# Two transformer blocks in fp32: the feed-forward up product as one 512-column product over both parts of the tokens, in four banks, with the gate product on GpSimd

## The chip, the core and the metric

One NeuronCore of a Trainium2 chip runs the whole program in one launch. The time is device microseconds from start to end of an execution; the profile gives a span, from the first instruction to the last. TensorE (PE) multiplies, VectorE (DVE), ScalarE (ACT) and GpSimd (POOL) do the elementwise work, SyncE (SP) issues all loads. PEld is TensorE's loading of the stationary operand, which overlaps its products.

## What is computed

256 tokens of width 1024 pass through a first block (an RWKV-7 and a dilated-attention mixer, then a gated feed-forward) and two layers of a second block, each with a feed-forward, a sparse-attention mixer and another feed-forward. That makes five feed-forwards. Cut to what matters here:

```python
D_FF = -(-8 * D_MODEL // (3 * 256)) * 256          # 2816

# first block
h = modulate(rms_norm(x, g_pre_ffn[i]), shift_f, scale_f)
u, gt = jnp.split(h @ w_ffn_in[i], 2, axis=-1)
f = (jax.nn.silu(u) * gt) @ w_ffn_out[i]
x = x + gate_f[:, None, :] * rms_norm(f, g_post_ffn[i])

# second block, twice in each of two layers
def swiglu(h, w13, w2):
    a, b = jnp.split(h @ w13, 2, axis=-1)
    return (jax.nn.silu(a) * b) @ w2
```

All of it is in float32.

## The kernel before

**Split products.** The feed-forward's products take operands of type fp32r. Each operand is split into a high part (ACT's copy into fp32r) and a low part (what that copy leaves of the fp32 value), and three products are added: high times high, high times low, low times high. For a feed-forward, the normed tokens `hT` are split once into `h_hi` and `h_lo`, and every weight is split as it arrives: ACT copies it into the high part (`high_up`, L1546; `high_down`, L1554), DVE subtracts to get the low part (`low_up`, L1984; L2006).

**Chunks.** The 2816 hidden channels are worked in FC = 11 chunks of 256. A chunk's up weights (2 MB, in one of two `ring` slots) hold 256 channels of u and 256 of the gate: four output tiles j of 128 channels (0 and 1 are u, 2 and 3 the gate). Each tile needs eight k-steps over the width of 1024, so a chunk has 32 of them. They come in two halves h of four k-steps, since `up_hi` and `up_lo` hold the weights of one half each: the second half is split while the first is multiplied. A k-step is three products of 256 columns (the tokens), L881, L882 and L883, each with a weight load of its own. The `down` products of a chunk (24 of 512 columns, L897 to L899) add onto banks 0 to 3 through all chunks.

**PSUM.** A chunk's up results take two banks, u in one and the gate in the other; even chunks use banks 4 and 5, odd ones 6 and 7. Chunk 0 is done unsplit (L854).

**Order.** Each engine runs its instructions in the order in which they are written, and waits on semaphores. PE's is up(0), up(1), down(0), up(2), down(1), up(3), ..., up(10), `down_end`. Before up(c) it waits for the gate product of the chunk that used the same banks (`act_ready`). For chunk c, in its loop:
- ACT: high part of the next chunk's first half (after the first half of up(c)); silu of u from PSUM (L1565); high part of the next chunk's second half; high part of the down weights (after down(c-1)).
- DVE: low part of the next chunk's first half; gate product from PSUM (L1995); high and low part of it (`act_hi` L1999, `act_lo` L2001); low part of the next chunk's second half; low part of the down weights (L2006); and, in the first four feed-forwards, four dot products for the conditioning vector of a later layer (`ada_layers`, L1953).

In `down_end`, PE multiplies half of chunk 9's down product, waits for `act_low` of chunk 10, runs eight products (L907, L908), waits for `dn_low`, and goes on (L910); then come norm, residual and the next stage, all of which wait for these sums. POOL has nothing to do in a feed-forward but the residual's add at its end (L2621). SP loads the up weights, the down weights and the dot products' weights in turn, each when its buffer is free.

Of the kernel before, what the change touches and what calls it, by code (L numbers as in the profile page):

```python
# [28 lines left out]
ACT = mybir.ActivationFunctionType  # L29
ALU = mybir.AluOpType  # L30
# [4 lines left out]
S = 256  # L35
NT = S // P
KD = D // P
FF = 2816
FC = FF // 256
# [239 lines left out]
def build(nc, T, out):  # L279
    with ExitStack() as ctx:  # L280
# [3 lines left out]
        def sem(name):  # L284
            return ctx.enter_context(nc.semaphore(name))
# [17 lines left out]
        silu = scratch[:, 1024:2048].rearrange("p (b n) -> p b n", b=2)  # L303
        fin = scratch[:, 2048:3072].rearrange("p (t n) -> p t n", t=2)
        with nc.sbuf_tensor("row_split", [P, D], F32R) as row_split:
            pass
# [22 lines left out]
        arena = sb("arena", [P, ARENA])  # L329
        h_hi, h_lo = (split[:, a:a + 2048].rearrange("p (k n) -> p k n", k=KD) for a in (0, 2048))  # L330
        up_hi, up_lo = (split[:, a:a + 4096].rearrange("p (h n) -> p h n", h=2) for a in (4096, 8192))
# [117 lines left out]
        up_high = sem("up_high")  # L449
        up_low = sem("up_low")  # L450
        dn_high = sem("dn_high")
        dn_low = sem("dn_low")
# [371 lines left out]
        def _(pe):  # L824
# [19 lines left out]
            def ffn_split(f, n, g):  # L844
# [21 lines left out]
                def up(c, i=0):  # L866
                    if c >= 2:
                        pe.wait_ge(act_ready, FC * f + c + i - 1)
                    if c == 0:
                        up_first()  # L870
                        return
                    if c == 1:
                        pe.wait_ge(h_low, 2 * (f + 1))
                    for h in range(2):
                        pe.wait_ge(up_low, up_count(f, c, h) + 2 * i)
                        for j in range(4):

                            dst = bank[4 + 2 * (c % 2) + j // 2][:, (j % 2) * S:(j % 2 + 1) * S]
                            for k in range(4):
                                a, kt_ = slice(k * 512 + j * P, k * 512 + j * P + P), 4 * h + k  # L880
                                mm(dst, up_hi[:, h, a], h_hi[:, kt_], start=(kt_ == 0 and j % 2 == 0), stop=False, skip_group_check=True)  # L881
                                mm(dst, up_hi[:, h, a], h_lo[:, kt_], start=False, stop=False, skip_group_check=True)  # L882
                                last = mm(dst, up_lo[:, h, a], h_hi[:, kt_], start=False, stop=(kt_ == KD - 1), skip_group_check=True)  # L883
                        last.then_inc(half_done, 1)
# [653 lines left out]
        def _(act):  # L1538
# [17 lines left out]
            def ffn_split(f, g):  # L1556

                def one(c, i=0):
                    if c < FC - 1:
                        high_up(f, g, c + 1, 0, i)  # L1560
                    if c == 0:
                        high_up(f, g, 1, 1)
                    act.wait_ge(half_done, 2 * FC * f + 2 * (c + 1) + 2 * i)
                    wait(act, act_ready, FC * f + c + i - 1 if c >= 2 else FC * f)
                    F(silu[:, c % 2], bank[4 + 2 * (c % 2)], ACT.Silu).then_inc(silu_ready, 1)  # L1565
                    if 0 < c < FC - 1:
                        high_up(f, g, c + 1, 1, i)
                    high_down(f, c, i)

                one(0)  # L1570
                one(1)
                if f == 0:
                    act.wait_ge(ang_ready, 1)
                    F(sin2[:], sin2[:], ACT.Sin)
                    F(cos2[:], cos2[:], ACT.Sin).then_inc(trig_ready, 1)
                with act.Fori(0, FC - 3, 2) as i:
                    one(2, i)
                    one(3, i)
                one(FC - 1)
# [366 lines left out]
        def _(dve):  # L1946
# [39 lines left out]
            def ffn_split(f, g, n, mods):  # L1986

                def one(c, i=0):
                    if c < FC - 1:
                        low_up(f, g, c + 1, 0, i)  # L1990
                    if c == 0:
                        low_up(f, g, 1, 1)
                    dve.wait_ge(silu_ready, FC * f + c + i + 1)
                    whole = act_t[:, c % 2].rearrange("p k n -> p (k n)")
                    tt(whole, silu[:, c % 2], bank[5 + 2 * (c % 2)], ALU.mult).then_inc(act_ready, 1)  # L1995
                    dve.wait_ge(act_ready, FC * f + c + i + 1)
# [4 lines left out]
                    tt(act_lo[:, c % 2], whole, act_hi[:, c % 2].bitcast(F32), ALU.subtract).then_inc(act_low, 1)  # L2001
                    if 0 < c < FC - 1:
                        low_up(f, g, c + 1, 1, i)
                    d_hi, d_lo = (up_hi[:, 1], up_lo[:, 1]) if c == FC - 1 else (dn_hi, dn_lo)
# [591 lines left out]
        def _(pool):  # L2596
# [20 lines left out]
            def add(n):  # L2617

                for t in range(NT):
                    pool.wait_ge(fin_read, 4 * n + 2 * t + 1)  # L2620
                    tt(x[:, t, 0:512], x[:, t, 0:512], fin[:, 0], ALU.add).then_inc(x_ready, 1)  # L2621

            def angles():

# [134 lines left out]
            add(0)  # L2759
            angles()  # L2760
            add(1)

            g(pool.memset(zb, 0.0))
            pool.memset(lf8, 0.0).then_inc(pool_zero, 1)

            for l in range(LAYERS):
                add(2 + 3 * l)
                channel_major(T2, CM_2 + 16 * l, Q1 + Q2 * l, range(14))
                for p in range(NP):
# [4 lines left out]
                    for e in range(2):  # L2774
# [3 lines left out]
                        last.then_inc(p_ready, 1)  # L2778
                add(3 + 3 * l)
                add(4 + 3 * l)  # L2780

# [17 lines left out]
```

## Time and profile before

| | |
|---|---|
| time, median of 3 runs | 1678.69 us (1675.34 to 1680.26) |
| span of the profiled execution | 1675.9 us |
| PE busy, mean granted clock over the span | 96%, 0.993 |
| the five feed-forwards from chunk 1 to the end of up(10) | 426 to 592, 622 to 788, 961 to 1126, 1154 to 1319, 1492 to 1658 us |

No time of its own is given for the profiled execution beside its span; the median lies 2.8 us above the span, and a difference worked out on the trace is applied to the median. A matmul's row shows a start and a modelled end, and products overlap: what one costs in a stream is the distance from its start to the next one's. "Busy" of PE thus says that it had work, not how fast it went. A row's "idle before" names what ended the wait.

### The profile page before, as it was taken

The numbers are of one execution on the slowest core, as the hardware profiler recorded it, in microseconds if no ns is written. First come the engines' busy times: TensorE is split into PE (matmuls) and PEld (weight loads), VectorE is DVE, ScalarE is ACT, GpSimd is POOL, SyncE is SP. The second block draws the span as 40 slices with busy tenths as digits, with TensorE's granted clock in tenths as the row PEclk, the third lists the DMA queues.
The fourth block names the chain that finished last, engine by engine and source line by source line (L and its number), as shares of the span: only waits on it lengthen the run. The fifth ranks groups of instructions, "written<-read, shape, count | busy, mean of one in ns | idle before, by whom it ended". The sixth has DMA issues, their size and how long they took to land.

```text
span 1675.9 us, 31948 instructions
## 1 busy us (share of the span) xinstructions
PE 1604.4 (96%) x13122; PEld 1447.5 (86%) x13122; DVE 1112.0 (66%) x1812; ACT 681.3 (41%) x1026; POOL 234.3 (14%) x291
## 2 busy tenths in 40 slices
PE   3999988999999999999999999999999999999998
PEld 3998778785999989999896899999999888699997
DVE  5986445474777767787657577876877666755554
ACT  3443423302433353333457433335333354743333
POOL 0531345032300000000016000000000002500000
PEclk9999979999999999999999999999999999999999
DMA  9963110276778829786640488765887563164531
GB/s 393 347 231 126 51 53 4 70 278 240 298 290 324 329 86 347 307 309 242 220 173 2 166 342 330 289 269 212 315 328 289 222 201 118 56 236 162 218 152 61
DMA packets 59544, 363.90 MB, mean 217 GB/s; under 512 B 14000, under 2 KB 14768, under 8 KB 39472
## 3 DMA queue, kind: packets, MB, share of 16 engines
q1 hardware_dynamic: 59440, 362.42, 56.9%
q8 instruction: 76, 1.25, 0.3%
q14 instruction: 28, 0.23, 0.1%
HBM read 361.32 MB, written 1.08 MB: 216 GB/s over the span
## 4 chain that ended last, share of the span: by engine, by line
PE 84%; DVE 7%; issue 3%; DMA 2%; ACT 2%; POOL 2%; SPq 0%; POOLq 0%; DVEq 0%; ACTq 0%
PE psum L883 11%; PE psum L882 11%; PE psum L881 11%; PE psum L897 5%; PE psum L898 5%; PE psum L899 5%; PE psum L854 4%; PE psum L950 2%; PE psum L1051 2%; PE psum L987 2%; PE psum L988 2%; PE psum L989 2%; DMA arena<-in_ada_head 2%; PE psum L1339 1%; PE psum L1340 1%
## 5 line engine op out<-in xcount | busy, mean ns | idle before, releaser
L881 PE MATMUL psum<-split 128*128 128x256 f32 x1600 | 453.0, 283 | 0.0
L883 PE MATMUL psum<-split 128*128 128x256 f32 x1600 | 452.8, 283 | 0.0
L882 PE MATMUL psum<-split 128*128 128x256 f32 x1600 | 452.8, 283 | 0.0
L882 PEld LDWEIGHTS psum<-split 128*128 128x128 f32 x1600 | 307.0, 192 | 1.8
L881 PEld LDWEIGHTS psum<-split 128*128 128x128 f32 x1600 | 307.0, 192 | 1.7
L883 PEld LDWEIGHTS psum<-split 128*128 128x128 f32 x1600 | 307.0, 192 | 0.0
L1984 DVE TENSOR_TENSOR split<-ring,split 128x2048 fp32r<-128x2048 f32 x100 | 228.6, 2290 | 70.9 <-ACT split L1546 67.4
L1546 ACT ACTIVATE split<-ring 128x2048 fp32r<-128x2048 f32 x100 | 190.8, 1912 | 192.9 <-PE psum L883 141.8
L2006 DVE TENSOR_TENSOR split<-ring_down,split 128x2048 fp32r<-128x2048 f32 x55 | 126.2, 2294 | 106.2 <-ACT split L1554 106.2
L1953 DVE CUSTOM_DVE_ANT_0 arena<-arena,c_row 128x1024 f32<-128x1024 f32 x144 | 167.6, 1220 | 0.0
L2621 POOL TENSOR_TENSOR x_res<-x_res,scratch 128x512 f32<-128x512 f32 x16 | 20.6, 1286 | 999.6 <-DVE scratch L2044 798.3
L1554 ACT ACTIVATE split<-ring_down 128x2048 fp32r<-128x2048 f32 x55 | 105.4, 1916 | 133.4 <-PE psum L899 133.4
L897 PE MATMUL psum<-split 128*128 128x512 f32 x400 | 156.3, 391 | 0.0
L898 PE MATMUL psum<-split 128*128 128x512 f32 x400 | 156.2, 391 | 0.0
L899 PE MATMUL psum<-split 128*128 128x512 f32 x400 | 155.6, 389 | 0.0
L1565 ACT ACTIVATE scratch<-psum 128x512 f32<-128x512 f32 x55 | 32.9, 598 | 209.9 <-PE psum L883 202.4
L899 PEld LDWEIGHTS psum<-split 128*128 128x128 f32 x400 | 75.1, 188 | 16.0
L897 PEld LDWEIGHTS psum<-split 128*128 128x128 f32 x400 | 75.3, 188 | 14.3
L898 PEld LDWEIGHTS psum<-split 128*128 128x128 f32 x400 | 75.3, 188 | 13.8
L854 PE MATMUL psum<-hT,ring 128*128 128x128 f32 x640 | 73.4, 275 | 4.8 <-DVE hT L2065 4.8
L1995 DVE TENSOR_TENSOR scratch<-scratch,psum 128x512 f32<-128x512 f32 x55 | 37.8, 687 | 60.3 <-ACT scratch L1565 60.3
L854 PEld LDWEIGHTS psum<-hT,ring 128*128 128x128 f32 x640 | 72.4, 192 | 6.0 <-issue 4.1
(446 smaller groups left out, 3020.6 us busy)
## 6 DMA issues: line engine op xcount, KB each, us to landing
ring<-in_up SPq DMA_DIRECT2D x55, 2048.0 KB, 10.2
arena<-in_ada SPq DMA_DIRECT2D x168, 512.0 KB, 6.4
ring_down<-in_down SPq DMA_DIRECT2D x55, 1024.0 KB, 4.9
ring<-in_in SPq DMA_DIRECT2D x19, 2048.0 KB, 8.9
ring<-in_gates SPq DMA_DIRECT2D x4, 2048.0 KB, 8.5
arena<-in_ada_head SPq DMA_DIRECT2D x4, 1536.0 KB, 18.7
ring_down<-in_w_out SPq DMA_DIRECT2D x3, 2048.0 KB, 12.4
ring<-in_w_out SPq DMA_DIRECT2D x3, 2048.0 KB, 11.0
```

The source lines that it names most:

```text
L854: last = mm(dst, w[:, k * 512 + j * P:k * 512 + j * P + P], hT[:, k, t * P:(t + 1) * P], start=(t == 0 and k == 0 and j % 2 == 0), stop=(k ...
L881: mm(dst, up_hi[:, h, a], h_hi[:, kt_], start=(kt_ == 0 and j % 2 == 0), stop=False, skip_group_check=True)
L882: mm(dst, up_hi[:, h, a], h_lo[:, kt_], start=False, stop=False, skip_group_check=True)
L883: last = mm(dst, up_lo[:, h, a], h_hi[:, kt_], start=False, stop=(kt_ == KD - 1), skip_group_check=True)
L897: mm(bank[2 * t + h], act_hi[:, c % 2, a], dn_hi[:, w], start=(c == 0 and k == 0), stop=False, skip_group_check=True)
L898: mm(bank[2 * t + h], act_hi[:, c % 2, a], dn_lo[:, w], start=False, stop=False, skip_group_check=True)
L899: last = mm(bank[2 * t + h], act_lo[:, c % 2, a], dn_hi[:, w], start=False, stop=False, skip_group_check=True)
L1546: F(up_hi[:, h], ring[:, (g + c) % 2, h * 2048:(h + 1) * 2048], ACT.Copy).then_inc(up_high, 1)
L1554: F(up_hi[:, 1] if c == FC - 1 else dn_hi, ring_down[:, c % 2], ACT.Copy).then_inc(dn_high, 1)
L1953: return dve.tensor_tensor_reduce(out=weights, in0=weights, in1=c_of, scale=1.0, scalar=0.0, op0=ALU.mult, op1=ALU.add, accum_out=out)
L1984: tt(up_lo[:, h], ring[:, (g + c) % 2, h * 2048:(h + 1) * 2048], up_hi[:, h].bitcast(F32), ALU.subtract).then_inc(up_low, 1)
L2006: tt(d_lo, ring_down[:, c % 2], d_hi.bitcast(F32), ALU.subtract).then_inc(dn_low, 1)
```

## The change

- PE: `h_hi` and `h_lo` now lie side by side for each k (`h_both`). A k-step is one product of the high weights with both parts (512 columns, a whole bank) and one of the low weights with the high part (256 columns, onto the first half of the same bank). The four tiles j of a chunk take banks 4 to 7, one each, so all chunks use the same four; the first half of each bank holds two of the three products, the second half the third (high weights times low tokens).
- ACT copies the second halves of the four banks to SBUF (`up_whole`, 1024 columns), waits for DVE, and takes silu from SBUF.
- DVE adds the four first halves onto that copy (`up_sum`), and moves the low part of the next weights (`low_up`) ahead of `act_hi`. It no longer does the gate product.
- POOL does the gate product from SBUF (`ffn_gated`).
- PE waits for `up_sum` of the chunk before, where it waited for the gate product of the one before that. Chunk 0 keeps its old path; in up(1) the tiles go 2, 3, 0, 1, with a wait for chunk 0's gate product ahead of tile 0.

```diff
@@ buffers
+        up_whole = scratch[:, 2048:3072]
...
-        h_hi, h_lo = (split[:, a:a + 2048].rearrange("p (k n) -> p k n", k=KD) for a in (0, 2048))
+        h_both = split[:, 0:4096].rearrange("p (k s n) -> p k s n", k=KD, s=2)
+        h_hi, h_lo = h_both[:, :, 0], h_both[:, :, 1]
@@ PE, up(c)
                     if c >= 2:
-                        pe.wait_ge(act_ready, FC * f + c + i - 1)
+                        pe.wait_ge(up_sum, (FC - 1) * f + c + i - 1)
...
-                        for j in range(4):
-
-                            dst = bank[4 + 2 * (c % 2) + j // 2][:, (j % 2) * S:(j % 2 + 1) * S]
+                        for j in ((2, 3, 0, 1) if c == 1 and h == 0 else range(4)):
+                            if c == 1 and h == 0 and j == 0:
+                                pe.wait_ge(act_ready, FC * f + 1)
                             for k in range(4):
                                 a, kt_ = slice(k * 512 + j * P, k * 512 + j * P + P), 4 * h + k
-                                mm(dst, up_hi[:, h, a], h_hi[:, kt_], start=(kt_ == 0 and j % 2 == 0), stop=False, skip_group_check=True)
-                                mm(dst, up_hi[:, h, a], h_lo[:, kt_], start=False, stop=False, skip_group_check=True)
-                                last = mm(dst, up_lo[:, h, a], h_hi[:, kt_], start=False, stop=(kt_ == KD - 1), skip_group_check=True)
+                                mm(bank[4 + j], up_hi[:, h, a], h_both[:, kt_].rearrange("p s n -> p (s n)"),
+                                   start=(kt_ == 0), stop=(kt_ == KD - 1), skip_group_check=True)
+                                last = mm(bank[4 + j][:, 0:S], up_lo[:, h, a], h_hi[:, kt_], start=False, stop=(kt_ == KD - 1), skip_group_check=True)
@@ ACT, one(c)
-                    wait(act, act_ready, FC * f + c + i - 1 if c >= 2 else FC * f)
-                    F(silu[:, c % 2], bank[4 + 2 * (c % 2)], ACT.Silu).then_inc(silu_ready, 1)
+                    if c == 0:
+                        wait(act, act_ready, FC * f)
+                        F(silu[:, 0], bank[4], ACT.Silu).then_inc(silu_ready, 1)
+                    else:
+                        act.wait_ge(act_ready, FC * f + c + i)
+                        F(up_whole.rearrange("p (j n) -> p j n", j=4), psum[:, 4:8, S:2 * S], ACT.Copy).then_inc(low_out, 1)
+                        act.wait_ge(up_sum, (FC - 1) * f + c + i)
+                        F(silu[:, c % 2], up_whole[:, 0:512], ACT.Silu).then_inc(silu_ready, 1)
@@ DVE, one(c)
-                    dve.wait_ge(silu_ready, FC * f + c + i + 1)
                     whole = act_t[:, c % 2].rearrange("p k n -> p (k n)")
-                    tt(whole, silu[:, c % 2], bank[5 + 2 * (c % 2)], ALU.mult).then_inc(act_ready, 1)
+                    if c == 0:
+                        dve.wait_ge(silu_ready, FC * f + 1)
+                        tt(whole, silu[:, 0], bank[5], ALU.mult).then_inc(act_ready, 1)
+                    else:
+                        dve.wait_ge(low_out, (FC - 1) * f + c + i)
+                        four = up_whole.rearrange("p (j n) -> p j n", j=4)
+                        tt(four, four, psum[:, 4:8, 0:S], ALU.add).then_inc(up_sum, 1)
+                        if c < FC - 1:
+                            low_up(f, g, c + 1, 1, i)
                     dve.wait_ge(act_ready, FC * f + c + i + 1)
...
-                    if 0 < c < FC - 1:
-                        low_up(f, g, c + 1, 1, i)
@@ POOL, new, called for each feed-forward
+            def ffn_gated(f):
+
+                def one(c, i=0):
+                    pool.wait_ge(silu_ready, FC * f + c + i + 1)
+                    if c >= 2:
+                        pool.wait_ge(act_low, FC * f + c + i - 1)
+                    else:
+                        wait(pool, act_low, FC * f)
+                    tt(act_t[:, c % 2].rearrange("p k n -> p (k n)"), silu[:, c % 2], up_whole[:, 512:1024], ALU.mult).then_inc(act_ready, 1)
+
+                one(1)
+                with pool.Fori(0, FC - 3, 2) as i:
+                    one(2, i)
+                    one(3, i)
+                one(FC - 1)
```

The start of up(1) in PE's own order, behind the unsplit products of up(0), before:

```order
L854 MATMUL psum<-hT,ring 128x128 x31
L881 MATMUL psum<-split 128x256 [waits up_low,h_low]
L882 MATMUL psum<-split 128x256
L883 MATMUL psum<-split 128x256
L881 MATMUL psum<-split 128x256
L882 MATMUL psum<-split 128x256
L883 MATMUL psum<-split 128x256
```

and after:

```order
L858 MATMUL psum<-hT,ring 128x128 x31
L885 MATMUL psum<-split 128x512 [waits up_low,h_low]
L887 MATMUL psum<-split 128x256
L885 MATMUL psum<-split 128x512
L887 MATMUL psum<-split 128x256
```

Six products of 256 columns for two k-steps became two of 512 and two of 256.

DVE's order over one chunk of the loop (`split<-ring` is `low_up`, `scratch<-scratch,psum` reads the up result, `split<-scratch` are `act_hi` and `act_lo`, `split<-ring_down` is the down weights' low part), before:

```order
L1984 TENSOR_TENSOR split<-ring,split 128x2048 [waits up_high]
L1993 REGISTER_ALU
L1995 TENSOR_TENSOR scratch<-scratch,psum 128x512 [waits silu_ready]
L1998 REGISTER_ALU [waits act_ready]
L1999 CAST split<-scratch 128x512 [waits down_done]
L2001 TENSOR_TENSOR split<-scratch,split 128x512 [waits act_high]
L1983 REGISTER_ALU
L1984 TENSOR_TENSOR split<-ring,split 128x2048 [waits up_high]
L2006 TENSOR_TENSOR split<-ring_down,split 128x2048 [waits dn_high]
```

and after:

```order
L1994 TENSOR_TENSOR split<-ring,split 128x2048 [waits up_high]
L2010 TENSOR_TENSOR scratch<-scratch,psum 128x1024 [waits low_out]
L1993 REGISTER_ALU
L1994 TENSOR_TENSOR split<-ring,split 128x2048 [waits up_high]
L2013 REGISTER_ALU
L2016 CAST split<-scratch 128x512 [waits down_done,act_ready]
L2018 TENSOR_TENSOR split<-scratch,split 128x512 [waits act_high]
L2021 TENSOR_TENSOR split<-ring_down,split 128x2048 [waits dn_high]
```

The 512-column product became a 1024-column sum that waits for ACT's copy, and the second `low_up` now stands right behind it.

ACT's order over the last chunk of the loop and the end of a feed-forward (`split<-ring` is `high_up`, `split<-ring_down` is `high_down`), before:

```order
L1546 ACTIVATE split<-ring 128x2048 [waits half_done]
L1563 REGISTER_ALU
L1565 ACTIVATE scratch<-psum 128x512 [waits act_ready,half_done]
L1546 ACTIVATE split<-ring 128x2048 [waits half_done]
L1553 REGISTER_ALU [waits down1_full]
L1554 ACTIVATE split<-ring_down 128x2048 [waits down_done]
L1576 REGISTER_ALU
L1576 COMPARE_AND_BRANCH
L1565 ACTIVATE scratch<-psum 128x512 [waits act_ready,half_done]
L1554 ACTIVATE split<-ring_down 128x2048 [waits half_done,down0_full]
```

and after:

```order
L1550 ACTIVATE split<-ring 128x2048 [waits half_done]
L1567 REGISTER_ALU
L1572 REGISTER_ALU [waits half_done]
L1573 ACTIVATE scratch<-psum 128x1024 [waits act_ready]
L1575 ACTIVATE scratch<-scratch 128x512 [waits up_sum]
L1550 ACTIVATE split<-ring 128x2048 [waits half_done]
...
L1586 REGISTER_ALU
L1586 COMPARE_AND_BRANCH
L1573 ACTIVATE scratch<-psum 128x1024 [waits act_ready,half_done]
L1575 ACTIVATE scratch<-scratch 128x512 [waits up_sum]
L1558 ACTIVATE split<-ring_down 128x2048 [waits half_done,down0_full]
```

Where one silu stood between the two `high_up`, there are now a copy, a wait for DVE's sum and a silu; the same at the end, ahead of `high_down`.

## Rows read from the trace of the kernel before

**Rows 1.** The page, part 1: busy time by engine.

```profile
PE 1604.4 (96%) x13122; PEld 1447.5 (86%) x13122; DVE 1112.0 (66%) x1812; ACT 681.3 (41%) x1026; POOL 234.3 (14%) x291
```

**Rows 2.** The page, part 4: the chain that ended last, by engine.

```profile
PE 84%; DVE 7%; issue 3%; DMA 2%; ACT 2%; POOL 2%; SPq 0%; POOLq 0%; DVEq 0%; ACTq 0%
```

**Rows 3.** Busy time in the five feed-forward blocks: the line that sums the stretches.

```profile
sum 828.00, PE 828.00 PEld 783.95 DVE 581.59 ACT 297.19 POOL 9.44; mean PE 165.60 PEld 156.79 DVE 116.32 ACT 59.44 POOL 1.89
```

**Rows 4.** Timeline of PE, first block: start us, us, then the instruction.

```profile
488.81 0.40 PE L897 MATMUL psum<-split 128*128 128x512 f32 x1
...
494.28 0.28 PE L881 MATMUL psum<-split 128*128 128x256 f32 x1
...
505.79 0.40 PE L897 MATMUL psum<-split 128*128 128x512 f32 x1
...
507.18 0.39 PE L897 MATMUL psum<-split 128*128 128x512 f32 x1
```

**Rows 5.** Timeline of PE in the second block's mixer: products of 284 columns.

```profile
830.72 0.29 PE L1353 MATMUL psum<-split 128*128 128x284 f32 x1
...
836.72 0.29 PE L1354 MATMUL psum<-split 128*128 128x284 f32 x1
```

**Rows 6.** Timeline of DVE, one chunk of the second feed-forward.

```profile
652.67 0.43 DVE L1999 CAST split<-scratch 128x512 fp32r<-128x512 f32 x1
...
653.74 2.28 DVE L1984 TENSOR_TENSOR split<-ring,split 128x2048 fp32r<-128x2048 f32 x1
658.57 2.29 DVE L2006 TENSOR_TENSOR split<-ring_down,split 128x2048 fp32r<-128x2048 f32 x1 [2.54 <-ACT split L1554]
660.77 1.22 DVE L1953 CUSTOM_DVE_ANT_0 arena<-arena,c_row 128x1024 f32<-128x1024 f32 x1
...
665.70 2.29 DVE L1984 TENSOR_TENSOR split<-ring,split 128x2048 fp32r<-128x2048 f32 x1
```

**Rows 7.** Timeline of ACT, the same chunk.

```profile
651.23 0.60 ACT L1565 ACTIVATE scratch<-psum 128x512 f32<-128x512 f32 x1 [3.19 <-PE psum L883]
651.72 1.91 ACT L1546 ACTIVATE split<-ring 128x2048 fp32r<-128x2048 f32 x1
```

**Rows 8.** Single lines: count, then duration ns min/median/max, first and last start.

```profile
L1670 ACT ACTIVATE raw<-psum x54: 362/386/388, 41.7 to 1416.0; 128x256 f32<-128x256 f32 x54
L1995 DVE TENSOR_TENSOR scratch<-scratch,psum x55: 679/687/690, 427.2 to 1657.6; 128x512 f32<-128x512 f32 x55
L2301 DVE TENSOR_SCALAR arena<-psum x1: 1757/1757/1757, 324.7 to 324.7; 128x1536 f32<-128x1536 f32 x1
L2621 POOL TENSOR_TENSOR x_res<-x_res,scratch x16: 1267/1288/1299, 395.3 to 1667.9; 128x512 f32<-128x512 f32 x16
L2607 POOL TENSOR_TENSOR pre<-raw x20: 616/1193/1720, 42.2 to 93.9; 128x256 f32<-128x256 f32 x20
```

**Rows 9.** Timeline of ACT, DVE and PE at the first block's end.

```profile
590.89 0.60 ACT L1565 ACTIVATE scratch<-psum 128x512 f32<-128x512 f32 x1 [9.60 <-PE psum L883]
591.59 0.69 DVE L1995 TENSOR_TENSOR scratch<-scratch,psum 128x512 f32<-128x512 f32 x1 [2.52 <-ACT scratch L1565]
592.31 0.43 DVE L1999 CAST split<-scratch 128x512 fp32r<-128x512 f32 x1
593.38 2.28 DVE L2006 TENSOR_TENSOR split<-ring_down,split 128x2048 fp32r<-128x2048 f32 x1
595.72 0.50 PE L910 MATMUL psum<-split 128*128 128x512 f32 x1
```

**Rows 10.** Timeline of PE and DVE, start of the fourth block's loop.

```profile
1165.49 0.40 PE L897 MATMUL psum<-split 128*128 128x512 f32 x1
1169.28 0.68 DVE L1995 TENSOR_TENSOR scratch<-scratch,psum 128x512 f32<-128x512 f32 x1
```

**Rows 11.** Timeline of PE in the first mixer, then windows with granted clock (PEclk).

```profile
221.53 0.68 PE L1189 MATMUL psum<-arena 64*64 64x64 f32 x16 [2.55 <-POOL arena L2708]
...
226.00:242.00 16.00, 15.98 (x259) 14.92 (x260) 7.71 (x21) 5.35 (x13) 7.83 (x11) 0.50 0.02 3
```

More of the change, by code:

```diff
@@ L450, in build @@
         up_low = sem("up_low")
+        low_out = sem("low_out")
+        up_sum = sem("up_sum")
         dn_high = sem("dn_high")
@@ L2760, in _ @@
             angles()
+            ffn_gated(0)
             add(1)
@@ L2766, in _ @@
             for l in range(LAYERS):
+                ffn_gated(1 + 2 * l)
                 add(2 + 3 * l)
@@ L2779, in _ @@
                 add(3 + 3 * l)
+                ffn_gated(2 + 2 * l)
                 add(4 + 3 * l)
```

## Prediction

> **What bounds the kernel now.** I read the busy times first: PE has work for 1604.4 of 1675.9 us [rows 1], and the chain that ended last is 84% PE [rows 2]. In the five feed-forward blocks PE is never without work, 828.00 of 828.00 us, while DVE has 581.59 and ACT 297.19 [rows 3]. So in the loop the time is the number of products times their distance, and an engine beside PE counts only if it makes PE wait. What one costs I take from starts in a stream [rows 4]. From L897 at 488.81 to L881 at 494.28 lie 24 down products, 5.47 us, 227.9 ns each; from there to L897 at 505.79 lie the 96 up products of 256 columns, 11.51 us, 119.9 ns each. A chunk takes 16.98 us. Twice the columns cost 108.0 ns more and not 119.9: some 12 ns come with each product, whatever its width. The 284-column products agree: 46 distances in 6.00 us, 130.4 ns, which is 10.5 ns more for 28 more columns (columns alone, at 108.0 ns for 256, would make 11.8) [rows 5]. The weight load isn't that charge, since a 512-column product has twice the time to hide it and pays it too.
>
> The exception is a block's end. There PE has only 12 products to do while silu, gate product, both parts of it and the low down weights are made one after another: silu at 590.89, gate product 591.59, `act_hi` 592.31, low down weights 593.38, and L910 starts at 595.72 when they are done [rows 9]. All that follows hangs on this chain, five times.
>
> **The change part by part.**
>
> *Products.* A k-step was 3 x 119.9 = 359.7 ns and becomes 227.9 + 119.9 = 347.8, or 11.9 less. There are 32 k-steps in a chunk, 10 split chunks, 5 feed-forwards: 1600, so -19.0 us, and a chunk takes 16.60 us. The mixed stream isn't in the trace. Its bounds: the first six down products behind up products stand 1.39/6 = 231.7 ns apart, and the later ones less, (494.28 - 488.81 - 1.39)/18 = 226.7 [rows 4]. If every 512 pays the first, a k-step is 351.6 and the saving 13.0 us; at the second, 346.6 and 21.0. I take the mean of a whole down block, between them.
>
> *The way from up(c) to up(c+1) in the loop.* Before, up(c+1) used other banks. Now it waits for the sum over the same ones, behind down(c-1), which gives 5.47 us of cover. What must fit: ACT's copy of 1024 columns, DVE's sum of 1024. ACT reads 256 from PSUM in 386 ns [rows 8] and 512 in 0.60 us [rows 7], 214 ns per 256, so 1.03 for 1024; above, two separate 512s make 1.20. DVE takes 0.687 for 512 and 1.757 for 1536 [rows 8], so 1.22 for 1024; above, 2 x 0.687 = 1.37. With an allowance of 0.35 for three hand-overs it is done 2.6 us after up(c), 2.9 before PE needs it. Cost nothing, while DVE is free at that moment.
>
> *Is it?* DVE now goes round in a closed loop: sum 1.27 with its hand-over; silu to `high_up` on ACT 0.49 and `high_up` 1.94 with hand-over [rows 7], in which DVE waits; `low_up` 2.20 (distance 658.57 to 660.77 of the same size); `act_hi` and `act_lo` 1.07 (652.67 to 653.74); low down weights 2.20; dot products 4.93 (660.77 to 665.70); `low_up` 2.20 [rows 6]. Sum 16.30 against PE's 16.60: 0.3 us per chunk to spare, 0.15 with the sum at its upper bound. The fifth block has no dot products. It also starts late in a block, when chunk 2's weights are still landing: in the worst, the fourth, DVE gets to its PSUM work at 1169.28, where down starts at 1165.49 [rows 10]. After: sum done 1170.55, PE there at 1165.49 - 0.38 + 5.47 = 1170.58. Just covered; price 0, at most 0.2. If the cover goes, each 0.1 us of DVE loop over 16.60 costs up to 36 x 0.1 us.
>
> POOL's product falls into DVE's wait for `high_up` and takes 1.29 alone [rows 8]; with chunks to spare before down(c) it costs nothing in the loop. The moved `low_up` ends 7.3 us behind up(c), needed at 5.47 + 5.56. SP issues the loads behind the same DVE steps, some 0.8 us later in each chunk; DMA is 2% of the chain [rows 2], and the buffers are two deep, so I count nothing for it.
>
> *Block end.* Here each added step is on the path [rows 9]. Out go silu to gate product 0.70 and gate product to `act_hi` 0.72: 1.42. In come copy 1.03, sum 1.22, silu 0.60, POOL's product 1.29 (L2621's, the same size [rows 8]) and four hand-overs, 0.30: 4.44. The rest is unchanged, and so L910 starts 3.02 us later in relation to up(10)'s end. Five times: +15.1 us. Bounds: 1.20 and 1.37 for the reads give +16.7; without hand-overs +13.6. Nothing starts earlier for it: DVE and ACT are both idle there before.
>
> *Chunk 0 and up(1):* tile 0 waits for chunk 0's gate product, done about 1.6 us after up(0), behind 8 k-steps (2.8 us). Nothing.
>
> **Sum:** -19.0 + 15.1 = -3.9 us. On the span 1675.9 that is 1672.0; on the median 1678.69 it is 1674.8, say 1675. With all bounds, -21.0 + 13.6 = -7.4 to -13.0 + 16.7 + 0.2 = +3.9. A measurement here tells about 0.3% or 5.0 us from no change, so the likeliest case lies within it, and reaches beyond on the faster side only.
>
> **Rivals.**
>
> *The charge isn't saved (slower).* The 12 ns may go with the work and not with the product: a mixed stream then costs 359.7 ns per k-step as before, and only the end's +15.1 is left: 1694. For it: no row has 512 and 256 in turn. Against: three widths fit one charge per product [rows 4, 5]. The Trainium skill (TensorE: Matmul & The Clock Gate, Back-to-back issue gap) gives columns over 2.4 GHz plus 2.5 ns, by which a merged product saves 2.5 ns; an estimate by it is -4.0 + 15.1 = +11.1 us, 1690. The trace disagrees on the charge, with 12.
>
> *PE's clock falls at the block ends (slower).* PE's 12 products (2.7 us) begin with the silu at 590.9 at the latest and are over by 593.6, about when `act_low` is made before (L2006 follows it at 593.38 [rows 9]); now it comes 3.02 later, and PE stands for about 3 us. In the first mixer it waited 2.55 us before 221.53, with little work ahead of that, and ran at half clock (0.50) through 226 to 242 [rows 11]. Behind the wait stand 36 products of 227.9 ns, 8.2 us; if half of them run at 1.2 GHz instead of 2.4 it is +4.1 us a block. One such fall cancels the gain; from three on the kernel is slower by over 0.3%; all five give +16.6, 1695. Against: here PE was full before and is full right after. By the same page (Part 1) an idle array is clocked down and a busy one gets its clock back; the trace shows both, at 222 and 244 us.
>
> *DVE's loop or POOL is slower than reckoned.* A loop of 16.9 instead of 16.30 makes PE wait 0.3 in most of 36 chunks, +8 after what slack there is: +4.1, 1683. Or POOL's product takes twice its time at the ends, +6.5: +2.6, 1681. POOL rows do range from 616 to 1720 ns for one size [rows 8]. Either stays within 0.3% of before; both together, or a loop over 16.95, are slower.
>
> *More is saved.* If in the mixed stream the short product's charge is hidden too (107.9 for 119.9), a further 19 us go: -23, 1656. PE would then need 16.2 us a chunk, DVE's loop of 16.30 takes over in four blocks (36 x 0.1 us back), and about -20 remains: 1659. For it I see only that the distance changes by 5 ns within a down block [rows 4].
>
> **Chances.** The forecast 0.64, charge not saved 0.06, clock 0.09, DVE or POOL 0.13, more saved 0.08. Of the forecast's range, -7.4 to +3.9 around -3.9, three eighths lie beyond -5.0. Faster by over 0.3%: 0.24 + 0.08 = 0.32. Slower: 0.06 + 0.06 + 0.05, and 0.02 for the forecast's tail: 0.19. Within: 0.49. The likeliest case's own range is 1671 to 1683. The range that should hold 8 in 10 takes in most of the rivals in the middle and leaves out "more saved" and the clock falling at four ends or more: 1668 to 1687.
>
> **What the profile would show.** Right: starts of L885 to L887 about 228 ns apart and of L887 to the next L885 about 120; a chunk of 16.6 us; PE busy through the loop with no wait on `up_sum`; copy 1.03, sum 1.22, POOL's product 1.29; L910 7.85 us after ACT's copy starts at a block's end, where it is 4.83 after the silu's start now. Wrong: PE waiting on DVE's sum L2010 in the loop, PEclk under 1 behind the ends, or other distances in the mixed stream. That last one is the largest unknown: each 5 ns per k-step are 8 us.

## The result: 0.6% slower, and the profile after

The changed kernel takes 1689.53 us in the median of 4 runs (1684.74 to 1692.5), the kernel before 1679.16 beside it; the ratio is 1.0058, with a 95% interval of 1.0042 to 1.0073, or 9.7 us more. The forecast was 1675.0 in a range of 1668 to 1687. The profiled execution is the fastest of the four (span 1683.0, mean granted clock 0.991; the others 0.987 to 0.989). Three single executions further down, far longer than all others (two of the kernel before, one of e6), count in no ratio, but the one of e6 is in its median of 1683.65.

Busy times of the page, after, which answer to [rows 1]:

```profile
PE 1597.1 (95%) x11522; PEld 1363.2 (81%) x11522; DVE 1134.1 (67%) x1812; ACT 733.5 (44%) x1076; POOL 299.1 (18%) x341
```

There are 1600 products fewer, but PE is busy only 7.3 us less, in a longer span. The first place to look is the loop. The timeline of ACT after, in the second feed-forward, gives the length of a chunk by the starts of its PSUM copy:

```profile
666.41 1.03 ACT L1573 ACTIVATE scratch<-psum 128x1024 f32<-128x1024 f32 x1 [3.80 <-PE psum L887]
683.20 1.03 ACT L1573 ACTIVATE scratch<-psum 128x1024 f32<-128x1024 f32 x1 [3.80 <-PE psum L887]
699.99 1.03 ACT L1573 ACTIVATE scratch<-psum 128x1024 f32<-128x1024 f32 x1 [3.80 <-PE psum L887]
```

A chunk takes 16.79 us: 0.19 less than the 16.98 of [rows 4], where 0.38 less was forecast. PE is never without work in it; this is the sum over five stretches inside the five blocks, to set beside [rows 3]:

```profile
sum 807.00, PE 807.00 PEld 688.34 DVE 595.92 ACT 336.80 POOL 67.50; mean PE 161.40 PEld 137.67 DVE 119.18 ACT 67.36 POOL 13.50
```

So the products themselves stand further apart than forecast. PE's timeline in the mixed stream:

```profile
655.18 0.40 PE L885 MATMUL psum<-split 128*128 128x512 f32 x1
655.41 0.28 PE L887 MATMUL psum<-split 128*128 128x256 f32 x1
655.53 0.40 PE L885 MATMUL psum<-split 128*128 128x512 f32 x1
...
656.59 0.40 PE L885 MATMUL psum<-split 128*128 128x512 f32 x1
```

From 655.18 to 656.59 lie four k-steps, 353 ns each; over a chunk's 32 it is 352.8 (11.29 us). In the mean of the whole trace 117 ns of it go to the product of 256 columns and 236 to that of 512. Forecast were 347.8, and at most 351.6. The down products behind the mixed stream are a little dearer too, 5.50 us for 24 where they took 5.47.

One place in the five blocks does wait, though a busy PE hides it (timeline of DVE and PE, first chunk of the fourth block's loop):

```profile
1173.02 1.21 DVE L2010 TENSOR_TENSOR scratch<-scratch,psum 128x1024 f32<-128x1024 f32 x1
1173.98 0.39 PE L903 MATMUL psum<-split 128*128 128x512 f32 x1
1174.37 0.49 PE L885 MATMUL psum<-split 128*128 128x512 f32 x1
```

DVE's sum ends at 1174.23, and L885 starts 0.39 us behind L903 instead of 0.23; that chunk takes 17.07 us, 0.28 more than the others. It is the tight spot that the prediction named, and it costs this once.

The end of the first block, which answers to [rows 9] (timeline after; starts and durations in us, then the instruction):

```profile
586.71 1.03 ACT L1573 ACTIVATE scratch<-psum 128x1024 f32<-128x1024 f32 x1 [9.31 <-PE psum L887]
587.84 1.22 DVE L2010 TENSOR_TENSOR scratch<-scratch,psum 128x1024 f32<-128x1024 f32 x1 [2.04 <-ACT scratch L1573]
589.09 0.63 ACT L1575 ACTIVATE scratch<-scratch 128x512 f32<-128x512 f32 x1 [1.36 <-DVE scratch L2010]
589.80 1.27 POOL L2646 TENSOR_TENSOR scratch<-scratch 128x512 f32<-128x512 f32 x1 [15.41 <-ACT scratch L1575]
591.11 0.43 DVE L2016 CAST split<-scratch 128x512 fp32r<-128x512 f32 x1 [2.04 <-POOL scratch L2646]
592.17 2.28 DVE L2021 TENSOR_TENSOR split<-ring_down,split 128x2048 fp32r<-128x2048 f32 x1
592.31 0.50 PE L911 MATMUL psum<-split 128*128 128x512 f32 x1 [2.86 <-DVE split L2018]
594.51 0.50 PE L914 MATMUL psum<-split 128*128 128x512 f32 x1
```

L914 (L910 before) starts 7.80 us behind the copy; 7.85 was forecast, and it was 4.83 behind the silu before. PE now stands idle for 2.86 us, and does so in all five blocks (waits of PE: line, releaser, total us, times, longest):

```profile
PE psum L911 <- DVE split L2018: 14.2, 5, 2.9
```

Behind that idle the granted clock falls in three of the five blocks. The second block's end, PE's timeline and two windows (the value before the DMA share is the clock):

```profile
789.49 0.80 PE L911 MATMUL psum<-split 128*128 128x512 f32 x1 [2.86 <-DVE split L2018]
790.08 0.63 PE L912 MATMUL psum<-split 128*128 128x512 f32 x1
...
791.36 0.63 PE L911 MATMUL psum<-split 128*128 128x512 f32 x1
```

```profile
788.00:792.00 4.00, 2.52 (x6) 2.03 (x7) 3.32 (x3) 2.18 (x3) 0.24 (x1) 0.59 0.02 4
792.00:796.00 4.00, 4.00 (x11) 3.11 (x11) 1.38 (x2) 0.00 (x0) 1.00 (x1) 0.55 0.00 0
```

The products stand 427 ns apart (790.08 to 791.36, three distances) where they stood 227: about half speed, the lower level of 1.2 GHz. From the copy at 783.88 to L914 at 793.07 it takes 9.19 us, 1.39 more than in the first block, and the four L914 products are slow as well (+0.8).

Block by block, the time from the first product behind up(10) to the 48th (all but the last few at the block's end) has grown by 2.98, 4.67, 3.97, 2.98 and 4.15 us against the trace before. So the longer chain costs 2.98 each time, and the lower clock 1.7, 1.0 and 1.2 us in the second, third and fifth block: 3.9 in this execution. A further fall, at 604 to 608 us (clock 0.57), lies behind a later wait, the one for the next stage's transposes; the kernel before has none there.

### The profile page after: what moved, and what is told of

Same layout as the page of the kernel before. It is cut to its first block, busy times and chain, and to the rows that moved or that the text cites. A ratio compares the mean times of both kernels' runs of the same rounds, so it can differ in the third digit from the quotient of the medians.

```text
span 1683.0 us, 29059 instructions
## 1 busy us (share of the span) xinstructions
PE 1597.1 (95%) x11522; PEld 1363.2 (81%) x11522; DVE 1134.1 (67%) x1812; ACT 733.5 (44%) x1076; POOL 299.1 (18%) x341
## 4 chain that ended last, share of the span: by engine, by line
PE 83%; DVE 7%; issue 3%; DMA 3%; ACT 2%; POOL 2%; SPq 0%; POOLq 0%; DVEq 0%; ACTq 0%
PE psum L885 22%; PE psum L887 11%; PE psum L901 5%; PE psum L903 5%; PE psum L902 5%; PE psum L858 4%; PE psum L954 2%; PE psum L1055 2%; DMA arena<-in_ada_head 2%; PE psum L1343 1%; PE psum L1344 1%; PE psum L1345 1%; PE psum L991 1%; PE psum L992 1%; PE psum L993 1%
## 5 line engine op out<-in xcount | busy, mean ns | idle before, releaser
L885 PE MATMUL psum<-split 128*128 128x512 f32 x1600 | 566.9, 398 | 0.0
L887 PE MATMUL psum<-split 128*128 128x256 f32 x1600 | 449.1, 281 | 0.0
L885 PEld LDWEIGHTS psum<-split 128*128 128x128 f32 x1600 | 300.6, 188 | 74.2 <-issue 0.4
L887 PEld LDWEIGHTS psum<-split 128*128 128x128 f32 x1600 | 302.1, 189 | 1.7
L2646 POOL TENSOR_TENSOR scratch<-scratch 128x512 f32<-128x512 f32 x50 | 64.7, 1294 | 826.7 <-ACT scratch L1575 826.7
L901 PE MATMUL psum<-split 128*128 128x512 f32 x400 | 157.5, 394 | 0.0
L903 PE MATMUL psum<-split 128*128 128x512 f32 x400 | 156.5, 391 | 0.0
L902 PE MATMUL psum<-split 128*128 128x512 f32 x400 | 156.1, 390 | 0.0
L1573 ACT ACTIVATE scratch<-psum 128x1024 f32<-128x1024 f32 x50 | 51.4, 1028 | 193.0 <-PE psum L887 192.9
L903 PEld LDWEIGHTS psum<-split 128*128 128x128 f32 x400 | 75.2, 188 | 17.3
L901 PEld LDWEIGHTS psum<-split 128*128 128x128 f32 x400 | 75.2, 188 | 16.5
L902 PEld LDWEIGHTS psum<-split 128*128 128x128 f32 x400 | 75.3, 188 | 14.5
L2010 DVE TENSOR_TENSOR scratch<-scratch,psum 128x1024 f32<-128x1024 f32 x50 | 60.9, 1218 | 37.8 <-ACT scratch L1573 37.7
L1575 ACT ACTIVATE scratch<-scratch 128x512 f32<-128x512 f32 x50 | 31.6, 632 | 87.6 <-DVE scratch L2010 87.6
L1963 DVE CUSTOM_DVE_ANT_0 arena<-arena 128x1024 f32<-128x1024 f32 x40 | 52.0, 1318 | 15.7 <-DMA arena<-in_ada_head 15.5
```

What stands on the lines that cost most here:

```text
L885: mm(bank[4 + j], up_hi[:, h, a], h_both[:, kt_].rearrange("p s n -> p (s n)"), start=(kt_ == 0), stop=(kt_ == KD - 1), skip_group_check=True)
L887: last = mm(bank[4 + j][:, 0:S], up_lo[:, h, a], h_hi[:, kt_], start=False, stop=(kt_ == KD - 1), skip_group_check=True)
L901: mm(bank[2 * t + h], act_hi[:, c % 2, a], dn_hi[:, w], start=(c == 0 and k == 0), stop=False, skip_group_check=True)
L902: mm(bank[2 * t + h], act_hi[:, c % 2, a], dn_lo[:, w], start=False, stop=False, skip_group_check=True)
L903: last = mm(bank[2 * t + h], act_lo[:, c % 2, a], dn_hi[:, w], start=False, stop=False, skip_group_check=True)
L1963: return dve.tensor_tensor_reduce(out=weights, in0=weights, in1=c_of, scale=1.0, scalar=0.0, op0=ALU.mult, op1=ALU.add, accum_out=out)
```

## The experiments

All ratios are against the kernel before, run on the same chip; 0.1% is 1.7 us.

| kernel | us, median | ratio, 95% interval | chunk in the loop, us |
|---|---|---|---|
| changed kernel | 1689.53 | 1.0058 (1.0042 to 1.0073) | 16.79 |
| e1, last chunk the old way | 1669.92 | 0.9943 (0.9931 to 0.9956) | 16.79 |
| e2, only last chunk new | 1697.14 | 1.0109 (1.0092 to 1.0126) | 16.98 |
| e3, grouped by width | 1678.31 | 0.9997 (0.9988 to 1.0007) | 16.57 |
| e4, filler at the ends | 1683.5 | 1.0029 (1.0018 to 1.0039) | 16.79 |
| e5, e1 and e3 together | 1660.14 | 0.9879 (0.9863 to 0.9896) | 16.57 |
| e6, grouped by four | 1683.65 | 1.0021 (1.0011 to 1.0031) | 16.69 |
| e7, staggered | 1684.32 | 1.0027 (1.0017 to 1.0038) | 16.72 |
| e8, e5 with gate product on DVE | 1685.27 | 1.0030 (1.0019 to 1.0040) | 16.57 to 17.55 |
| e9, e5 with fewer passages | 1660.61 | 0.9887 (0.9871 to 0.9903) | 16.55 |
| e10, real work in the idle | 1690.49 | 1.0064 (1.0042 to 1.0086) | 16.79 |

**e1 and e2: the middle against the end.** In e1, chunk 10 keeps the form of before; its silu and gate product read PSUM directly:

```diff
+ if c == FC - 1:
+     dst = bank[4 + j // 2][:, (j % 2) * S:(j % 2 + 1) * S]
+     mm(dst, up_hi[:, h, a], h_hi[:, kt_], ...)
+     mm(dst, up_hi[:, h, a], h_lo[:, kt_], ...)
+     last = mm(dst, up_lo[:, h, a], h_hi[:, kt_], ...)
+     continue
```

> Chunks 1 to 9 of each block in the new form, chunk 10 as in the kernel before. Theory A (the mixed stream saves only 6.4 ns a k-step, 359.7 to 353.3; the 3.0 us at each block's end come from the longer chain behind the last chunk; the clock falls come from the idle that this chain leaves): 1440 k-steps x 6.4 ns = 9.2 us saved, no added chain, no falls: 9 us less than before, about 1670, ratio 0.9945, chunk period 16.79 us, PE waiting under 0.1 us ahead of the last down block, granted clock 1.00 at all five ends. Rival B (the added work on ScalarE, VectorE and GpSimd holds the loop up, so that the chunks of the middle carry part of the loss): 1675 or more and a period over 16.8 us. Rival C (the charge is not saved at all): 1679, as before.

Measured: 9.6 us less than before, with a chunk of 16.79 us (45 x 0.19 would be 8.6; the interval reaches from 7.4 to 11.6). Of L911's wait nothing is left, and no window behind a wait at a block's end has a clock under 1.00.

e2 is the reverse: only chunk 10 takes the new form.

> Chunks 1 to 9 as before, only chunk 10 of each block in the new form. Theory A: five chains of +3.0 us = +15.1, less 160 k-steps x 6.4 ns = 1.0, plus what the clock falls cost (0 to 6 us): 1693 to 1699, ratio 1.0085 to 1.012; L914 again 7.8 us behind the copy's start and PE idle 2.9 us ahead of it. If the loss came from the loop of the middle chunks instead (rival B), it would be near before: 1679 to 1684.

Measured: 18.3 us more than before, 4.2 beyond the 15.1 - 1.0 expected without falls of the clock. PE waits at the ends as after (waits of PE in e2, then windows behind the second, third, fourth and fifth block):

```profile
PE psum L917 <- DVE split L2025: 14.2, 5, 2.9
```

```profile
796.00:800.00 4.00, 3.11 (x9) 2.46 (x10) 3.00 (x3) 1.59 (x3) 0.00 (x0) 0.74 0.00 0
1140.00:1144.00 4.00, 4.00 (x13) 3.14 (x12) 1.89 (x3) 0.00 (x0) 0.06 (x1) 0.66 0.00 0
1336.00:1340.00 4.00, 4.00 (x12) 3.14 (x13) 2.46 (x2) 0.67 (x2) 0.00 (x0) 0.66 0.00 0
1680.00:1684.00 4.00, 4.00 (x15) 3.17 (x14) 1.29 (x3) 0.07 (x1) 1.29 (x1) 0.75 0.00 0
```

The clock falls here with 45 of 50 chunks in the old stream: the falls come with the idle, not with the mixed products. Middle and end are two separate effects, and the end is the loss.

**e4 and e10: the clock.** e4 adds twelve products ahead of the wait; their values are dropped:

```diff
  down_half(FC - 2, 0)
+ pe.wait_ge(up_sum, (FC - 1) * (f + 1))
+ for _ in range(12):
+     mm(bank[5], act_hi[:, 1, 0:P], dn_hi[:, 0:512], start=True, stop=True, ...)
  pe.wait_ge(act_low, FC * f + FC)
```

> The changed kernel with 12 products of 512 columns into bank 5 (free by then, their values are dropped) in the stretch in which TensorE waits at each block's end, behind the sum of chunk 10. Theory A (the idle of 2.86 us makes the granted clock fall): TensorE idles 0.2 us instead of 2.86 ahead of L911 of after, the clock stays 1.00 at all five ends, every run is near 1684 and their spread is below 2 us; the chain's 3.0 us stay. Rival (the falls have another cause, such as the load of the mixed stream): falls stay at the ends and the median is 1689 to 1691 as after.

Measured: 1683.5. Timeline of PE at the first block's end (L923 are the filling products), and windows there:

```profile
591.85 2.90 PE L923 MATMUL psum<-split 128*128 128x512 f32 x12
594.89 0.50 PE L911 MATMUL psum<-split 128*128 128x512 f32 x1
```

```profile
588.00:592.00 4.00, 4.00 (x21) 3.32 (x20) 1.54 (x4) 1.38 (x2) 0.00 (x0) 1.00 0.00 0
592.00:596.00 4.00, 3.86 (x18) 2.84 (x17) 2.28 (x3) 3.67 (x5) 1.30 (x1) 1.00 0.02 4
596.00:600.00 4.00, 3.92 (x18) 2.90 (x17) 1.67 (x4) 1.56 (x5) 0.00 (x0) 1.00 0.00 0
```

PE does useless work instead of standing, on the same chain, and the kernel is 0.29% (4.9 us, by the two ratios) faster than the changed one. The clock stays at 1.00 behind all five ends. One fall is left, later, at 604 to 612 us, where PE waits for the next stage's transposes, as after. The spread was not below 2 us as expected but 5 (1682.29 to 1687.4; eight of nine runs within 2.5). That 2.86 us of idle costs more than 2.86 us is what the Trainium skill (TensorE: Matmul & The Clock Gate, Part 1) leads one to look for, since by it an idle array is clocked down; this case's rows agree, though not in every block.

e10 puts real work in that place, chunk 9's products for the second 128 tokens:

```diff
  down_half(FC - 2, 0)
+ down_half(FC - 2, 1).then_inc(down_done, 1)
  pe.wait_ge(act_low, FC * f + FC)
...
- down_half(FC - 2, 1).then_inc(down_done, 1)
```

> The changed kernel with real work in place of the fillers of e4: the 12 products of chunk 9 for the second 128 tokens stand ahead of the wait for chunk 10's low part instead of behind its products for the first 128. TensorE no longer idles ahead of L911 of after, but what follows hangs on the first 128 tokens' chain, which starts as late as before the edit, so the 2.8 us come back as idle ahead of the transposes (L841, idle 1.0 to 3.8 us). Expected: as e4, 1683.5, if the clock stays up, 1686 to 1690 if it now falls behind the later idle; the gain of the full 2.7 us a block, 1671 to 1676, only if the second tokens' chain is what the next stage waits for.

Measured: 1690.49. The idle and the fall have only moved, ahead of and behind the next stage's transposes (timeline, then windows of e10; the clock is under 1 there in all five blocks):

```profile
608.01 1.97 PE L841 MATMUL psum<-const,xn 128*128 128x128 f32 x8 [3.67 <-DVE xn L2045]
```

```profile
608.00:612.00 4.00, 2.44 (x10) 2.06 (x11) 1.48 (x5) 2.74 (x9) 0.00 (x0) 0.50 0.92 327
612.00:616.00 4.00, 4.00 (x21) 4.00 (x21) 2.92 (x5) 2.50 (x6) 2.41 (x3) 0.50 0.00 0
```

The work to bring forward would have to be that of the first 128 tokens, on which all that follows hangs; it is the work that waits.

**e3, e6, e7, e9: where the other half of the saving went.** e3 gives the same products in another order (in outline):

```diff
- for j in ...: for k in range(4): 512 columns, 256 columns
+ for j in ...: for k in range(4): 512 columns
+ for j in ...: for k in range(4): 256 columns
```

> The changed kernel with the products of each half chunk regrouped: 16 of 512 columns, then 16 of 256 (2 changes of width instead of 32); the block ends are as after. Theory D (the dear product is a charge of about 6.5 ns per change back to 512 columns): 346.6 + 0.4 ns per k-step, 6.3 ns x 1600 = 10 us less than after, about 1679. Theory E (a run-in: the first six or so 512-column products of a group cost 233 ns, the rest 226.7, as in the down blocks): 4 ns x 1600 = 6.5 us less than after, about 1683. Theory F (512-column products with these weights cost 233.6 ns whatever stands between them): as after, 1689.5.

Measured: 1678.31, 0.6% under the changed kernel. PE's timeline of e3, a chunk's four groups (the third in the row that begins it: 16 products of each width per half):

```profile
655.05 3.79 PE L886 MATMUL psum<-split 128*128 128x512 f32 x16
658.68 2.08 PE L891 MATMUL psum<-split 128*128 128x256 f32 x16
660.59 3.82 PE L886 MATMUL psum<-split 128*128 128x512 f32 x16
664.25 2.08 PE L891 MATMUL psum<-split 128*128 128x256 f32 x16
666.16 0.40 PE L905 MATMUL psum<-split 128*128 128x512 f32 x1
```

A product of 512 columns takes 3.63/16 = 226.9 ns, one of 256 takes 1.91/16 = 119.4, and a k-step (666.16 - 655.05)/32 = 347.2. These are close to the forecast's numbers (347.8; 16.60 us a chunk, here 16.57). So the 12 ns do go with each product, and the merger saves them; the alternation of widths gives about half back.

e6 groups by four (one tile: 4 of 512, 4 of 256), e7 lets each 256-column product lag its partner by four, so that it adds to another bank:

> The changed kernel with the products of one tile regrouped by four: 4 of 512 columns, then 4 of 256, into the same bank. Mixed stream: 353.3 ns a k-step with 16 changes of width and back in a half chunk; grouped: 347.2 with one. A charge of 6.5 ns per change gives 346.8 + 6.5/4 = 348.4 ns, a period near 16.63 us and 1681. A run-in of several products behind each change leaves all four at the dear price: 353 ns, 16.79 us, 1689.

> The changed kernel with each 256-column product lagging its 512-column product by four (one tile, another bank): widths alternate in 12 of 16 places, but no product adds to the columns that the one before it has written, nor reads the same moving columns. If the charge is for the change of width: 346.8 + 6.5 x 13/16 = 352.1 ns, 16.75 us, 1688. If it is for following a product on the same bank and columns, or for the shared moving data: 347 ns, 16.58 us, 1679.

Measured: 16.69 and 16.72 us a chunk. In the traces the up products of a chunk take 11.20 and 11.25 us, or 350.0 and 351.7 ns a k-step, where the strict alternation takes 352.8. e7 rules out the shared bank and moving data, which would have given 347. e6 fits neither theory: a fixed charge per change would give 16.63, a full price on all four 16.79.

The starts in e3's trace show what happens, in the mean of its 50 first groups of 512 columns behind 256: the first five products take 233.5, 235.8, 228.5, 232.6 and 230.4 ns, and from the sixth on it is 227. That is a run-in, 27 ns together. The other way round a little comes back: the first two products of 256 columns behind 512 take 113.4 and 119.1 ns, then 120, so 7.5 less. In the strict alternation every 512 is a first one (236) and so is every 256 (117), which leaves 6 ns a k-step above the 346.8 of each width alone (226.8 and 120.0). With groups of four it is (350.0 - 346.8) x 4 = 13 ns a group.

e9 tests that, on the kernel of e5 below, which has e3's order and e1's last chunk: the second half turns its order round, so that a chunk has one passage from 256 to 512 columns and not two.

```diff
+ for part in ((low, high) if h else (high, low)):
+     last = part(js)
```

> The kernel of e5, with the order by width turned round in the second half of each chunk 1 to 9: 512s, 256s | 256s, 512s, and then the 512-column down products. A chunk then has one passage from 256 to 512 columns instead of two. From the groups of e6 and e3, each passage costs 6.5 ns (one 512-column product behind it), some 15 (four) or 30 (sixteen), a run-in and no fixed charge. So one passage less is worth 0.03 us a chunk: a period of 16.54 us, 1.4 us less in all, which the time (1658.8) hardly shows and the period does. If the dear products come from something else in the mixed stream, the period stays 16.57.

Measured: a chunk of 16.55 us against 16.57 (27 ns less for one run-in and 7.5 more for one way back make 0.02), and this in PE's timeline, a chunk's three groups and the first down products:

```profile
655.06 3.79 PE L896 MATMUL psum<-split 128*128 128x512 f32 x16
658.68 4.00 PE L904 MATMUL psum<-split 128*128 128x256 f32 x32
662.52 3.82 PE L896 MATMUL psum<-split 128*128 128x512 f32 x16
666.17 0.39 PE L923 MATMUL psum<-split 128*128 128x512 f32 x1
...
667.53 0.39 PE L923 MATMUL psum<-split 128*128 128x512 f32 x1
```

The down products behind 512-column ones are 1.36/6 = 227 ns apart from the first on; behind 256-column ones the first six were 231.7 [rows 4]. In time it can't be told from e5. What in TensorE makes the run-in stays open; the runs show where it comes, not why.

**e5 and e8: the better kernel, and VectorE's room in it.**

> The two edits together: chunks 1 to 9 in the new form with the products of a half grouped by width (16 of 512 columns, then 16 of 256), chunk 10 as in the kernel before. Period of a chunk 16.57 us as in the grouped kernel against 16.98 of before, 45 chunks x 0.41 = 18.5 us, no added chain, no clock falls at the ends: 1661, ratio 0.989. If the 0.22 us a chunk of the grouped kernel came from fewer idle-born falls and not from the stream, it would stay at 1668 to 1670.

Measured: 1660.14, ratio 0.9879: 20.3 us less than before, 1.2%. With e9, which can't be told from it, it is the fastest of all, and PE waits at its block ends no more than before.

> The kernel with both edits (e5), its gate product of chunks 1 to 9 moved from GpSimd to VectorE. The prediction put VectorE's closed loop at 16.30 us in the four blocks that also carry the modulation dot products; with 0.69 us more it is 16.99, above TensorE's 16.57, and VectorE becomes the bound in these 36 chunks: +0.42 x 36 = 15 us on e5, about 1676; in the fifth block (no dot products) nothing. If the loop had much more room than 0.3 us, the time stays that of e5, 1661.

Measured: 25.1 us more than e5, where 15 was expected. In the fifth block, which has no dot products, the chunk stays at 16.57; in the others the first three or so are at 16.6 too (the slack of the start), and then (in the first block from the fifth on) they take 17.11 to 17.55, 17.28 in the mean. These periods add up to 15.6 us of the 25.1; that this is near the 15 of the expectation is luck, for fewer chunks were slow, each by more. DVE's timeline of e8, one chunk of the second block:

```profile
704.36 2.29 DVE L2011 TENSOR_TENSOR split<-ring,split 128x2048 fp32r<-128x2048 f32 x1
706.57 1.21 DVE L2029 TENSOR_TENSOR scratch<-scratch,psum 128x1024 f32<-128x1024 f32 x1
710.29 2.29 DVE L2011 TENSOR_TENSOR split<-ring,split 128x2048 fp32r<-128x2048 f32 x1 [2.50 <-ACT split L1564]
712.50 0.68 DVE L2033 TENSOR_TENSOR scratch<-scratch 128x512 f32<-128x512 f32 x1
...
721.89 2.29 DVE L2011 TENSOR_TENSOR split<-ring,split 128x2048 fp32r<-128x2048 f32 x1 [0.34 <-issue]
```

The closed loop shows itself: DVE's only long wait is the 2.50 us for ACT's high part, which hangs on DVE's own sum. Without the product's 0.69 it is 17.28 - 0.69 = 16.59 us, where the forecast reckoned 16.30; 0.34 of it, every second chunk, is the turn of the hardware loop, which the sum left out (0.17 a chunk; the other 0.12 is not traced). The late DVE delays the ends of the first four blocks too, where PE waits 6.9 us in all, and the clock falls behind one of them. The other 2 us or so are not traced.

## Why the prediction was wrong, step by step

The account, in us, from the periods, the chain and the runs:

| | forecast | measured |
|---|---|---|
| products, 50 chunks | -19.0 | 50 x -0.19 = -9.5 |
| block ends, the chain | +15.1 | 5 x (7.80 - 4.83) = +14.9 |
| DVE's sum, start of the fourth block | 0, at most +0.2 | +0.3 |
| clock behind the ends | 0 | +3.9 in the profiled execution; +4.9 as the changed kernel less e4, +4.2 in e2 |
| sum | -3.9 | +9.6 with 3.9, +10.6 with 4.9; measured 9.7 by the ratio |

The two traces bear the sum out: from the first down product of the first block (437.87 before, 435.37 after) to the end they differ by 9.6 us. The 2.5 us in which the spans differ less (1683.0 - 1675.9 = 7.1) lie ahead of it, almost wholly in stages that the change doesn't touch. e4 tests the first two terms apart from the clock: -9.5 + 14.9 = 5.4, measured 4.9.

- **Products: the mis-sized term.** The step that failed is the stream's price, "I take the mean of a whole down block, between them" [rows 4], and its upper bound of 351.6 too. That mean is of 24 products of one width, of which only the first five are dear; in the mixed stream each 512-column product is the first behind another width and costs 236, above even the six, while the 256-column one costs 117: 352.8 ns a k-step for 347.8, and 9.5 us saved for 19.0. The mechanism, a charge per product and not per column, was right, and e3 has 347.2 ns for the forecast's 347.8. The rival "charge isn't saved" and, with it, the 2.5 ns that the Trainium skill (TensorE: Matmul & The Clock Gate, Back-to-back issue gap) puts between products, are refuted by e3 (359.7 - 347.2 = 12.5 ns a merger), five times the page's gap. The page gives that gap for an isolated product and has other spacings for a stream of weight loads and products, about 131 ns for 512 columns; the 226.8 here don't agree with those either.
- **Clock: a rival given 0.09, and it came true in part.** Its idle was forecast at about 3 us and is 2.86. It was priced at 4.1 us a block, half of the products behind the wait at the lower level; it costs 1.0 to 1.7 us where it comes, and in the traces with the long chain and no filling work it comes at two (e6) to five (e7) of the ends. The "against" was the wrong step: "here PE was full before and is full right after" did not keep the clock up.
- **Block end: right**, in each link (copy 1.03, sum 1.22, POOL's product 1.27) and in the sum.
- **The covers: right but for one place.** PE waits for the sum only in the first chunk of the fourth block's loop, some 0.3 us, where the prediction saw it just covered and allowed 0.2. But **DVE's closed loop** has some 0.2 us of room under 16.79 and next to none under 16.57 (e8), not 0.3: two slips, a loop reckoned 0.29 too short and a PE reckoned too fast, hid each other, which is luck.
- **Chances.** Slower by over 0.3% had 0.19. With the products at their true price and the clock at full speed it is +0.3% (e4, 1683.5, inside the stated range); only with the second miss on the same side does the time leave it.

## What to carry to other kernels

Merging products saves a fixed charge each, but keep products of one width together: strict alternation gave back about half of it. A longer way from PSUM to the next operand is free in the middle of a pipeline and paid in full where it drains, so peel the last chunk and leave it the short way; both together turned 0.6% slower into 1.2% faster. And price an idle of TensorE with the clock behind it, above all where what it waits for is the head of everything that follows.

## What the hardware showed beyond expectation

- The run-in: behind products of 256 columns the first five of 512 cost 27 ns more than 5 x 226.8 (e3, e9, and the down products of the kernel before), while the first two of 256 behind 512 cost 7.5 less (e3). In strict alternation that is 236 and 117 ns. Nothing here shows why.
- An idle of 2.86 us in a stream that was full on either side brought the clock to half speed for some microseconds in three of five places in one execution (first products 427 ns apart), and not in the other two, for the same instructions and the same idle.
- At the lower clock the charge per product isn't seen: 427 ns are 512 columns at 1.2 GHz and nothing more, while the 227 at the upper level are 13 above 512 columns at 2.4 GHz.
